# Cache pages of six sequences laid on 64 partitions each, with two queues writing opposite halves

## The reference, cut to what matters

```
past = cache_pool[page_table].reshape(b, past_len, MLA_ROW)
c_past, kr_past = past[..., :KV_LORA], past[..., KV_LORA:]
s_past = (einsum('bthc,bkc->bhtk', q_lat, c_past) + einsum('bthr,bkr->bhtk', q_rope, kr_past)) * MLA_SCALE
p = softmax(concatenate([s_past, s_new], axis=-1))
o_lat = einsum('bhtk,bkc->bthc', p[..., :past_len], c_past) + ...
```

## Time and profile before

| | us |
|---|---|
| median of 3 runs | 1802.79 (1801.79 to 1802.81) |
| profiled execution | 1799.03 |
| its span | 1797.4 |

### The profile page before, as it was taken

One profiled execution on the slowest core, in us unless ns is written; L12 is line 12 of the kernel. 1 busy time (PEld: TensorE's weight loads), 2 busy tenths in 40 slices (PEclk: granted clock), 3 DMA queues, 4 the chain that ended last, 5 costly groups with the idle time before them and its releaser, 6 DMA issues.

```text
span 1797.4 us, 27863 instructions
## 1 busy us (share of the span) xinstructions
PE 1685.7 (94%) x9786; PEld 828.5 (46%) x9787; DVE 652.6 (36%) x1597; ACT 380.8 (21%) x878; POOL 218.6 (12%) x313
## 2 busy tenths in 40 slices
PE   7899889989899999999998999999999999999995
PEld 5466665545444444443433444555444444334331
DVE  2334488832322222222211656764322222212213
ACT  2233345521111111111100234341111111101012
POOL 1232024400000101010001200000001010101010
PEclk9899999999999999999999999999899999999997
DMA  6153049784479999999997700123899999999984
GB/s 186 52 156 110 27 149 305 254 316 178 169 308 417 416 420 414 417 421 412 423 408 328 275 1 13 69 85 138 323 403 414 421 416 419 414 419 412 413 359 153
DMA packets 84883, 513.81 MB, mean 286 GB/s; under 512 B 20821, under 2 KB 43302, under 8 KB 58586
## 3 DMA queue, kind: packets, MB, share of 16 engines
q1 hardware_dynamic: 66378, 463.45, 64.1%
q0 software_dynamic: 18416, 49.16, 8.4%
HBM read 499.65 MB, written 26.52 MB: 293 GB/s over the span
## 4 chain that ended last, share of the span: by engine, by line
PE 71%; DMA 16%; DVE 6%; issue 2%; ACT 2%; DVEq 1%; SPq 1%; ACTq 0%; POOLq 0%
PE ps L2072 64%; DMA mem<-in_moe_w_up 13%; PE ps L2077 7%; ACT mem L790 2%; DMA mem<-in_cache_mla 1%; DVE mem L1355 1%; DMA mem<-in_x_sample 1%; SPq L478 1%; DVE mem L1850 0%; DMA mem<-moe_rows_back 0%; ACTq L967 0%; DVE mem L1821 0%; DMA mem<-in_mla_wq_b 0%; DVE mem L1813 0%; DVE mem L1814 0%
## 5 line engine op out<-in xcount | busy, mean ns | idle before, releaser
L2072 PE MATMUL ps<-mem 128*64 128x512 f32 (+14 forms) x8402 | 1520.7, 479 | 66.3 <-DMA mem<-in_moe_w_up 16.9
L2072 PEld LDWEIGHTS ps<-mem 128*64 128x64 f32 (+5 forms) x8402 | 665.3, 147 | 836.1 <-issue 744.6
L790 ACT ACTIVATE mem<-ps 128x512 f32<-128x512 f32 (+7 forms) x358 | 193.2, 545 | 559.5 <-PE ps L2072 386.0
L2077 PE MATMUL ps<-mem 64*128 64x64 f32 (+3 forms) x1384 | 202.7, 281 | 37.9 <-DMA mem<-in_x_prompt 6.7
L2077 PEld LDWEIGHTS ps<-mem 64*128 64x128 f32 (+3 forms) x1384 | 168.2, 182 | 124.2 <-issue 96.9
L1689 DVE TENSOR_TENSOR mem<-mem,ps 64x512 f32<-64x512 f32 x64 | 44.2, 690 | 434.1 <-ACT mem L1033 434.0
L727 POOL DMA_INDIRECT moe_rows_back<-mem x64 | 57.3, 895 | 844.0 <-DVE mem L1707 833.5
L1033 ACT ACTIVATE mem<-ps 64x512 f32<-64x512 f32 x64 | 37.6, 588 | 555.1 <-PE ps L2072 555.1
L1707 DVE COPY mem<-ps 64x512 f32<-64x512 f32 x64 | 44.3, 693 | 146.0 <-PE ps L2072 146.0
L1355 DVE STREAM_TRANSPOSE mem<-mem 128x2560 f32<-128x2560 f32 x32 | 89.2, 2824 | 16.2 <-DMA mem<-in_cache_mla 15.9
L677 POOL DMA_DIRECT2D mem<-in_cache_mla x96 | 51.5, 536 | 76.2 <-PE ps L2072 69.0
(11 more groups left out here) (240 smaller groups left out, 517.7 us busy)
## 6 DMA issues: line engine op xcount, KB each, us to landing
mem<-in_moe_w_gate SPq DMA_DIRECT2D x64, 2048.0 KB, 21.4
mem<-in_moe_w_up SPq DMA_DIRECT2D x64, 2048.0 KB, 28.2
mem<-in_moe_w_down SPq DMA_DIRECT2D x64, 2048.0 KB, 19.4
mem<-in_cache_mla POOLq DMA_DIRECT2D x160, 160.0 KB, 3.8
mem<-in_cache_mla SPq DMA_DIRECT2D x96, 160.0 KB, 4.6
mem<-moe_rows_back SPq DMA_DIRECT2D x8, 1024.0 KB, 8.9
mem<-in_mla_wkv_b SPq DMA_DIRECT2D x8, 512.0 KB, 5.6
mem<-in_mla_wo SPq DMA_DIRECT2D x1, 4096.0 KB, 14.2
```

The lines of the kernel that those rows point to most:

```text
L790: return act.activation(out, in_, ACT.Copy)
L2072: return pe.matmul(out, lhsT, rhs, start=start, stop=stop)
L2077: return pe.transpose(out, in_, ident[at:at + n, at:at + n])
```

## The change

For sequences 2 to 7 a page goes to 64 partitions, two neighbouring rows (2560 B, contiguous in the cache) to a partition. Page j and its neighbour j+1 (j even) share the columns of both: one takes partitions 0 to 63, the other 64 to 127. SP's even pages go to the lower half and its odd ones to the upper; POOL's the other way round. The number of transfers, their order, who issues them, the waits and the semaphores are as before. The transposes, scores and values read the same addresses as before; only which row lies where is different. Sequences 0 and 1 keep the old layout.

```diff
+        def page_rows(b, j, upper, page):
+
+            at = j // 2 * 2 * ROW
+            return (pages_flat[b % 2][P // 2 * upper:P // 2 * (upper + 1), at:at + 2 * ROW],
+                    a["cache_mla"][0][bass.ds(page, 1)].rearrange("a (p r) c -> p (a r c)", r=2))
+
...
-                    sp.dma_start(pages[b % 2][:, j, :], a["cache_mla"][0][bass.ds(at[n], 1)].rearrange("a p c -> p (a c)")
+                    sp.dma_start(*page_rows(b, j, j % 2, at[n])
                                  ).then_inc(sig[f"pages{b % 2}" if n < 8 else f"third_pages{b % 2}"], DMA)
...
-                    g.dma_start(pages[b % 2][:, j, :], a["cache_mla"][0][bass.ds(at[n], 1)].rearrange("a p c -> p (a c)")
+                    g.dma_start(*page_rows(b, j, 1 - j % 2, at[n])
                                 ).then_inc(sig[f"late_pages{b % 2}" if n < 8 else f"fourth_pages{b % 2}"], DMA)
```

## The result

The changed kernel took 1826.09 us at the median of 4 runs (1819.40 to 1829.94) against 1802.29 for the kernel before: a ratio of 1.0121, 95% interval 1.0102 to 1.0141. (The ratios here are estimates over the runs with their intervals. They need not be the quotient of the medians, which is 1.0132 for this pair.) The profiled execution is the shortest of the four, 1819.40 us with a span of 1817.7, against 1799.03 and 1797.4: +20.4 us.

What follows compares the result with a forecast made beforehand. The page stage was taken as bound by PE and ACT (8.18 us a part) beside DMA (8.04). Slower half-partition writes +27 us, less 3 for packets, made +24: 1823 profiled, 1826 us median, range 1800 to 1852.

Steps and rivals of the forecast that it cites:

- Two limits side by side: Page stage: PE and ACT need 8.18 us a part, DMA 8.04; only 3.5 to 4 us of waits on the path.
- The half: Pages written to one half of the partitions: engines hold each other up, 0.75 of 326 GB/s, +27 us.
- the small load: x_sample load to 32 partitions in the trace before: DMA rate per busy engine fell by a factor of 0.53.
- the gather: Gather to at most 64 partitions of one half beside the experts' weights: 427 GB/s fell to mean 318, factor 0.75.
- The sum: Page stage, 12 parts: +27 us for the slower rate, less 3 for packets, gives +24; median 1826 us.
- The whole rest moves: Behind the page stage: nothing wins the loss back, since SP's next loads wait for the last values.
- the signs that I named: Changed profile: 245 to 255 GB/s, share 0.97+, steps near 10.3 us, DVE waits 30+ us, PE gaps about 2 us.
- The packets: SP's page queue: fewer, larger packets save 0 to 5.8 us of DMA time, 3 us taken.
- The issue: Page transfers issued by SP and POOL: faster issue worth 0, at most 1 us over the stage.
- Balance: Rival, chance 0.24: page loads to opposite halves keep all ways in use; 1799 to 1806 us, likeliest 1801.
- Turns: Rival, chance 0.16: page loads run at one half's rate, 215 to 202 GB/s; 1840 to 1855 us.
- The estimate of 208 GB/s: Page stage, from the skill's 6% gain for two transfers at once: 151 us, +50 us.

Runs made afterwards that it cites:

- the three half-load runs: Kernel before with only rows 0 to 63 of each page of sequences 2 to 7 loaded, to three partition placements; 1799.13, 1804.53 and 1800.74 us.
- the run with wide transfers: Kernel before with two neighbouring fixed pages per transfer, 2560 B pieces on 128 partitions, page table not followed for sequences 2 to 7; 1800.46 us, ratio 0.9977.
- half_lower: Kernel before, loading only rows 0 to 63 of each page of sequences 2 to 7, always to partitions 0 to 63; 1799.13 us.
- half_middle: Kernel before, loading only rows 0 to 63 of each page of sequences 2 to 7, always to partitions 32 to 95; 1804.53 us.
- even_odd: Changed kernel with each page on every second partition, its neighbour on the others, instead of one half; 1805.62 us, ratio 1.0003.
- same_half: Changed kernel with POOL's page j sent to the same half as SP's, not the opposite one; 1829.33 us, ratio 1.0144.

## Why the prediction was right

**Two limits side by side.** Right. The floor of 8.18 us a part from the earlier trace rows makes 106.3 us for 13 steps; the three half-load runs came to 105.5. I had put at most 3.5 to 4 us on the path; the floor gives 4.2, and the run with wide transfers won 4 (3.3 of them within the stage, 106.42 against 109.75). So the 15.9 us of DVE's waits were indeed mostly slack.

**The half.** Right in kind, and the factor I took was near: 0.75 of 326 GB/s. Measured, rate over share, were 268 / 1.04 = 258 and 253 / 1.05 = 241 GB/s, factors of 0.79 and 0.74. (Taken over the share, as I had done for the small load, the gather's own factor is 327 of 423 GB/s, 0.77; I had divided rates alone.) The gather of the earlier trace rows was thus the better guide than the small load of the earlier trace rows, whose 0.53 nothing here came near to; the lowest was 0.70, with small pieces in halves (228 / 1.00 of 324). Both rows had shown transfers into part of the partitions; what they could not show, that it is where the partitions lie and not how many there are, the run on every second partition did. That agrees with the Trainium skill, page SBUF — State Buffer, "Door 1: The DMA port swizzle", by which 64 partitions from 0 reach half of the ports and partitions on both sides of 64 reach more. No run shows the ports or which engines meet.

**The sum.** That the median came out within 0.1 us of the 1826 that I took is luck. The sum put +24 us on the stage; it gave +16.9 in the first profiled execution and +22.2 in the repeated one. The forecast steps of near 10.3 us were 9.80 and 10.18. The term of the half was thus sized too high for the first of the two and about right for the second, as their rates are: 268 and 253 GB/s in the views, against 245. "The whole rest moves" by one amount holds as far as can be seen: the 4.1 and 6.0 us that both executions had more behind the stage lie within what the other executions show there. Of the signs that I named, DVE's waits (33.9 us, all 12 parts), the share (1.04) and SP's packets (6,144 less) came; PE's gaps did not come as named, with 0.2 to 1.7 us before 13 of the turns and up to 2.9 us before the scores, where I had looked for none.

**The packets.** I took 3 us of DMA time out of 0 to 5.8. In the run on every second partition the rate over share is 308 / 0.90 = 342 against 324, 5% better, some 5 us of DMA time for the stage, near my upper end if all of it is due to the packets; POOL's queue, whose packets did not get fewer, became a little faster too (44.7% for 12.19 MB from 260 to 340 us, against 47.1% for 12.49). But none of it reached the time there (1.0003), where only the 4.2 us above the floor could be won and pages came no sooner to DVE: it waited 17.5 us, against 15.9.

**The issue.** Wrong in sign: the only case I bounded was a faster issue of 64 pieces. SP took 145 ns more for each. It was priced at nothing, and nothing is what it cost in the run on every second partition.

**The rivals.** Balance, which I gave 0.24, turned out true in the half-load runs and false in the change; the point from which it would decide, an efficiency over 0.92, was not reached with 0.74 to 0.79. Turns, at 215 GB/s, did not come either: even with both queues on one half the rate was 249. The Trainium skill's section "Can I just issue two DMAs to hit both halves?" of the page SBUF — State Buffer says that two transfers at once, one to each half, moved only 6% more than one alone. No run here has one queue alone; the nearest, opposite halves against the same half, gave 253 and 268 for 249 GB/s, 2% and 8% more, which is of that size. The estimate of 208 GB/s that I drew from the page did not hold.

## What to carry to other kernels

Before making a transfer cheaper, find the floor that the other engines set: here 4 of 16 us of waiting could be won, and it stood beside a DMA load of 95% that any loss of efficiency would push over. When a tile is laid on 64 partitions, take ones that lie on both sides of 64 and not one half. With every second one the same instruction ran at the full rate of 308 GB/s; 32 to 95 was tried at half the load only, where it cost a share of 0.58 against 0.72. One queue on a half is enough to spoil both. Two queues on opposite halves balanced while the DMA engines had room and did not when they were the bottleneck, which is when it was wanted.

## What the runs showed that I had not expected

SP's issue of one 160 KB transfer depends on its shape: 345 ns for 128 pieces of 1280 B on 128 partitions, 490 for 64 of 2560 B on 64, 619 for 128 pieces on 64 partitions. It is not the bytes: 64 pieces of 1280 B on partitions 0 to 63 took 490 ns too, and on 32 to 95 it was 539 (half_lower, half_middle). POOL's goes another way: 536, 518 and 589 ns.

One queue on halves beside one on all partitions is as bad as both on halves (1.0111 with SP's alone) or worse (1.0184 with POOL's alone). The other queue's packets slow down too, at 5.1% and 5.3% of the DMA engines' time a MB against 3.8%, so a queue cannot be kept out of it. Why the loss is not smaller than with both on halves was not settled: an uneven demand on the halves fits these two but not the run with both queues on the same half.

In the stretch from 255 to 345 us PE's mean granted clock follows how long the stage is. It was 1.00 in all runs with up to 112.2 us from part 2's turns to part 15's, 0.98 with 126.6 (the change), 0.96 with 129.1 to 134.4, and 0.92, 0.91 and 0.89 with 136.0, 141.0 and 147.6 (SP's pages alone, POOL's alone, small pieces), where PE waits longest. What this added in all was not priced; one place shows it, in the change's timeline above: behind the wait of 2.87 us the 40 products at 266.65 took 4.02 us at a granted clock of 0.57, where 40 of the same form took 2.39 us at 1.00 before the wait and behind it. Behind the stage no such order is seen: the 194 products took 54.80 us in the change and in half_lower, 55.30 in even_odd, and 52.66 in the kernel before and in same_half. A difference of 2 to 4 us there, found in one pair of profiles, says nothing of a change.
